# Query and gate products of the sparse attention in one four-bank buffer, and two modulation steps moved

## The reference, cut to what matters

```
def mixer_a(x, w_in, w_o, positions):
    proj = x @ w_in                      # x is 256 x 2048
    q, k, v, gate, iq, ik, iw = jnp.split(proj, SPLITS_A, axis=-1)
    ...                                  # rotary positions, indexer, top-k, softmax attention: o
    return (o * jax.nn.silu(gate)) @ w_o
```

```
mod_l = (jax.nn.silu(c) @ w_ada[l] + b_ada[l])[:, None, :]
sh_a, sc_a, gt_a, sh_f, sc_f, gt_f = jnp.split(mod_l, 6, axis=-1)
```

## Time and profile before

| | us |
|---|---|
| median of 3 runs | 2222.39 |
| lowest, highest | 2218.21, 2222.41 |
| the profiled execution, its own time | 2220.76 |
| its span in the profile | 2219.0 |
| TensorE busy (share of the span) | 2169.6 (98%) |
| VectorE busy | 1539.7 (69%) |
| ScalarE busy | 1044.7 (47%) |

### The profile page before, as it was taken

One profiled execution on the slowest core, in us unless ns is written; L12 is line 12 of the kernel. 1 busy time (PEld: TensorE's weight loads), 2 busy tenths in 40 slices (PEclk: granted clock), 3 DMA queues, 4 the chain that ended last, 5 costly groups with the idle time before them and its releaser, 6 DMA issues.

```text
span 2219.0 us, 34255 instructions
## 1 busy us (share of the span) xinstructions
PE 2169.6 (98%) x14840; PEld 1979.5 (89%) x14840; DVE 1539.7 (69%) x1894; ACT 1044.7 (47%) x1124; POOL 42.2 (2%) x81
## 2 busy tenths in 40 slices
PE   6999999999999999999999999999999999999998
PEld 3798887999888888888888899999999998899998
DVE  3579987889897566665667877965677645655674
ACT  3355353334554345543454444545345436764353
POOL 0000100000000000000000000000000000000000
PEclk8999998999999999999999999999999999999999
DMA  9968865786675555555555454434544554345543
GB/s 405 403 247 321 325 264 209 284 324 228 264 287 211 188 189 190 188 189 190 189 190 201 160 190 152 171 134 157 185 170 177 186 190 171 133 155 188 179 164 132
DMA packets 64791, 470.48 MB, mean 212 GB/s; under 512 B 7200, under 2 KB 7200, under 8 KB 8320
## 3 DMA queue, kind: packets, MB, share of 16 engines
q1 hardware_dynamic: 55008, 398.16, 48.8%
q0 software_dynamic: 9488, 68.03, 8.0%
q10 hardware_dynamic: 144, 2.10, 0.2%
HBM read 466.16 MB, written 2.10 MB: 211 GB/s over the span
## 4 chain that ended last, share of the span: by engine, by line
PE 88%; DVE 7%; DMA 2%; ACT 1%; issue 1%; SPq 0%; DVEq 0%; ACTq 0%
PE acc L2198 59%; PE aux L2198 29%; DVE ada_acc L1182 2%; DVE lo L1162 2%; DMA raw<-stream 1%; DMA ada_raw<-stream 1%; ACT hi L488 1%; DMA ada_raw<-ada_stream 0%; PE aux L2754 0%; DVE conv_sum L1483 0%; DVE columns L1457 0%; DVE ada_acc L1179 0%; DVE rstd L2102 0%; DVE rstd L1305 0%; PE aux L2556 0%
## 5 line engine op out<-in xcount | busy, mean ns | idle before, releaser
L1162 DVE TENSOR_TENSOR lo<-raw,hi 128x2048 fp32r<-128x2048 f32 x337 | 769.8, 2288 | 422.5 <-ACT hi L488 422.1
L488 ACT ACTIVATE hi<-raw 128x2048 fp32r<-128x2048 f32 x337 | 643.2, 1911 | 681.6 <-PE acc L2198 499.8
L2198 PE MATMUL acc<-act_both,hi 128*128 128x256 f32 (+1 forms) x5696 | 871.1, 308 | 17.3 <-ACT hi L488 5.3
L2198 PEld LDWEIGHTS acc<-act_both,hi 128*128 128x128 f32 x5696 | 777.1, 193 | 70.5 <-issue 18.7
L2198 PE MATMUL acc<-act_both,lo 128*128 128x256 f32 x3408 | 454.0, 284 | 0.0
L2198 PEld LDWEIGHTS acc<-act_both,lo 128*128 128x128 f32 x3408 | 435.7, 193 | 7.3 <-issue 0.2
L2198 PE MATMUL aux<-act_both,hi 128*128 128x512 f32 (+1 forms) x1248 | 258.2, 355 | 0.0
L2198 PEld LDWEIGHTS aux<-act_both,hi 128*128 128x128 f32 x1248 | 207.6, 190 | 29.6
L1182 DVE SCALAR_TENSOR_TENSOR ada_acc<-ada_raw,silu_c,ada_acc 128x512 f32<-128x512 f32 x224 | 152.7, 744 | 1.4 <-DMA ada_raw<-ada_stream 1.2
L2198 PE MATMUL aux<-act_both,lo 128*128 128x256 f32 x1040 | 138.7, 283 | 0.0
L2198 PEld LDWEIGHTS aux<-act_both,lo 128*128 128x128 f32 x1040 | 134.3, 191 | 4.6 <-issue 0.2
(11 more groups left out here) (357 smaller groups left out, 1713.7 us busy)
## 6 DMA issues: line engine op xcount, KB each, us to landing
raw<-stream SPq DMA_DIRECT2D x361, 1024.0 KB, 4.8
ada_raw<-ada_stream POOLq DMA_DIRECT2D x64, 1024.0 KB, 5.5
ada_raw<-stream SPq DMA_DIRECT2D x12, 1024.0 KB, 12.5
x<-x_t SPq DMA_DIRECT2D x1, 2048.0 KB, 7.6
ctx<-ctx_t SPq DMA_DIRECT2D x1, 2048.0 KB, 19.9
x<-x_t ACTq DMA_DIRECT2D x1, 2048.0 KB, 10.1
out<-x SPq DMA_DIRECT2D x3, 512.0 KB, 7.6
p_raw<-p_t POOLq DMA_DIRECT2D x1, 512.0 KB, 3.7
```

What stands on the lines that cost most here:

```text
L488: nc.scalar.activation(HI[high_slot(c)][:, :], RAW[SLOT[c]][:, :], ACT.Copy).then_inc(hi_done, 1)
L1162: V.tensor_tensor(LO[SLOT[c]][:, :], RAW[SLOT[c]][:, :], HI[high_slot(c)][:, :].bitcast(F32), ALU.subtract)\
L2198: return TE.matmul(out, lhs, rhs, start=start, stop=stop, skip_group_check=True)
```

## The change

Layer a takes layer b's way. Its query groups 1 to 3 and gate groups 0 to 2 go through `one_buffer`; ScalarE's and VectorE's steps 16, 20, 24, 28, 32 and 36 take the tiles over with `sides_out` and `sides_in`; the tag-dependent branches fall away; `single` now counts six groups of layer a ahead of layer b's. The third gate group gets its SiLU in step 37 from a copy. In `ADA_STEPS` the entries 7 and 8 go and 30 and 31 come, so that every modulation chunk from the fifth to the 37th runs in a later step than before; by the rule of `REDUCE_AT` the sums of groups 9 to 12 move from chunks 12, 14, 16 and 18 to 13, 15, 17 and 20, and that of group 16 from 29 to 32.

```
-ADA_STEPS = sorted([4, 4, 5, 5, 7, 8, 10, 11] + [m for m in range(12, 43) if m not in (30, 31)] +
-                   [12, 13, 14, 15, 16, 17, 18, 20, 24, 27, 28])
+ADA_STEPS = sorted([4, 4, 5, 5, 10, 11] + list(range(12, 43)) + [12, 13, 14, 15, 16, 17, 18, 20, 24, 27, 28])
...
     def single(tag, n):
-        return n
+        return n if tag == "a" else n + 6
...
                 for m in range(42):
                     first(m)
-                    if apart and m == 12:
+                    if m == 12:
                         act_evac(gq, U[:, 0:4, :])
-                    if apart and m in (16, 20, 24):
+                    if m in (16, 20, 24):
                         sides_out(m // 4 - 4, U[:, m - 12:m - 8, :])
-                    if apart and m in (28, 32, 36):
+                    if m in (28, 32, 36):
                         sides_out(m // 4 - 4, U[:, KD + m - 28:KD + m - 24, :])
                     split(c0 + m + 2)
...
-                    if not apart and 12 <= m <= 24 and m % 4 == 0:
-                        g = m // 4 - 3
-                        act_evac(gq + g, U[:, 4 * g:4 * g + 4, :])
-                    if not apart and m in (28, 32):
-                        g = m // 4 - 7
-                        act_evac(gg + g, U[:, KD + 4 * g:KD + 4 * g + 4, :])
...
-                    if m == 35 or (apart and m == 37):
+                    if m in (35, 37):
...
-                    if m == 40 or (not apart and m == 36):
+                    if m == 40:
...
-                    if q4 < (3 if tag == "b" else 2):
+                    if q4 < 3:
...
                 for m in range(42):
                     first(m)
-                    if tag == "b" and m in (16, 20, 24):
+                    if m in (16, 20, 24):
                         sides_in(m // 4 - 4, U[:, m - 12:m - 8, :])
-                    if tag == "b" and m in (28, 32, 36):
+                    if m in (28, 32, 36):
                         sides_in(m // 4 - 4, U[:, KD + m - 28:KD + m - 24, :])
                     split(c0 + m + 2)
...
-            phase("q_a", 4, after=attend_a)
-            phase("gate_a", 4, after=attend_a)
+            projections("a", "q_a", "gate_a", attend_a)
```

More of the change, by code:

```diff
@@ L937, in mixer @@
                 gv, gq, gg = PH[v][1], PH[q][1], PH[gate][1]
-                apart = tag == "b"
                 def sides_out(w, dst):
```

## The result

| | before | after |
|---|---|---|
| median | 2222.40 us (2218.21 to 2225.91, 6 runs) | 2233.14 us (2230.06 to 2236.06, 6 runs) |
| ratio to the kernel before | | 1.0051 (95%: 1.0039 to 1.0063) |
| the profiled execution | 2220.76 us | 2236.06 us |

The change costs 0.5%, 10.7 us between the medians. The two profiled executions lie 15.3 us apart, and it is these 15.3 us that the traces can divide. The one of the kernel after is the longest of its six, 2.9 us over their median.

A forecast was written before the change was run, and what follows sets the result against it. TensorE, working in 98% of the span, was taken as the bound. Layer a's +25.6 us less 8 for modulation gave +17.6: 2238.4 us for the profiled execution, 2240 for the median, range 2227 to 2250.

The forecast's parts named there:

- waits at 16, 20: Layer a, chunks 16 and 20: TensorE waits 4.4 and 5.0 us for adds because VectorE's queue is behind.
- waits at 24, 28, 32: Layer a, steady handovers: VectorE's adds stand behind `maximum2`, which waits for scores; TensorE waits 2.2 us each, 6.6 in all.
- wait at 36: Layer a, step 36: ScalarE's copies stand behind `head_out`, so TensorE waits 1.8 us.
- slower clock: Layer a: four of six possible waits lower TensorE's clock, 3.1 us per fall, +12.4 us; bounds zero and six falls.
- shorter products: Layer a, six groups of four chunks: each chunk 0.19 us shorter, 4.6 us less in all (2.4 to 5.3).
- layer a: Handovers 17.8 us less 4.6 for products, plus 12.4 for clock falls: +25.6 us.
- modulation: First block: later chunks remove two waits for sums and two clock falls, partly lost before norms: -8 us (0 to -11.5).
- Rival 2: Layer a's handover is as smooth as layer b's, where TensorE was never seen waiting: 2209.8 us; chance 0.07.
- Rival 1: The clock stays up after all of layer a's handovers: 2227.6 us; chance 0.13.
- Rivals 3 and 4: 3: VectorE's queue swallows the modulation gain, 2248 us, chance 0.10; 4: only steps 16, 20, 36 cost, 2227.2 us, 0.06.

The follow-up runs named there:

- e3: The changed kernel with layer a's hand-over (VectorE's adds, ScalarE's copies) put ahead of everything else in steps 16 to 36: 2218.50 us, ratio 0.9994.
- e5: The changed kernel with only VectorE's adds put ahead of everything else in steps 16 to 36, ScalarE's order kept: 2222.07 us, one run.
- e4: As e3, with VectorE's adds of the first two wide groups moved into steps 15 and 19, ScalarE's copies of the second into 19: 2209.40 us, 0.9953.
- e6: The changed kernel with half of the rounds of the top-k choice left out, so other keys are chosen: 2225.24 us, one run.
- e12: e4 with the query rotations spread over steps 13, 14, 17, 20, 22, 24, 25 and 26: 2208.69 us, ratio 0.9942.
- e1: The kernel before with only the new list of modulation steps: 2213.99 us, ratio 0.9966.
- e10: The kernel before with modulation entries 7 and 8 kept and only the nine chunks of steps 24 to 29 moved one step later: 2214.07 us, 0.9958.
- e2: The changed kernel with the old list of modulation steps, so the wide groups alone: 2241.36 us, ratio 1.0090.
- e8: e4 with 6, 5 and 4 idle VectorE instructions ahead of the adds of steps 24, 28 and 32: 2226.42 us, one run.
- e9: e4 with query rotations moved from steps 17, 18 to 20, 21 and from 21, 22 to 22, 23: 2213.79 us, ratio 0.9967.
- e7: e4 with 4, 5 and 6 idle VectorE instructions ahead of the adds of steps 24, 28 and 32: 2228.61 us, one run.
- e11: e9 with the smaller modulation edit of e10 in place of the whole new list: 2217.64 us, ratio 0.9977.

## Why the prediction was right in its sign, point by point

| term | forecast | measured in the profiled execution |
|---|---|---|
| waits at 16, 20 | 4.4, 5.0 | 4.23, 4.70 |
| waits at 24, 28, 32 | 2.2 each | 1.92 each |
| wait at 36 | 1.8 | 1.54 |
| slower clock | 4 falls x 3.1 = 12.4 | 3 falls: 2.4 + 1.6 + 1.6 = 5.6 |
| shorter products | -4.6 | -2.7 |
| layer a | +25.6 | +19.1 |
| modulation | -8 | -6.6 |
| up to 170 us | 0 | +2.8 |
| sum, profiled execution | +17.6 | +15.3 |
| between the medians | +17.6 | +10.7 |

- **The waits held.** All six came at the places named and within 0.3 us of the sums of single rows. The steady ones were 0.3 shorter: from `maximum2` to the adds it took 1.32 us as in the earlier trace rows, but `maximum2` began 0.04 us after TensorE was free (1456.88 - 1.92 = 1454.96) and not 0.38 after. e3 and e5 show the mechanism, e4 and e6 that of chunks 16 and 20.
- **The step that was mis-sized is the price of one fall of the clock.** I took 3.1 us from the first block, where two waits came one after the other with short products between them; whether that is why a fall cost more there no run tested. Behind a single wait in a stretch of dense products it was 1.6 us in eleven cases and 2.2 to 2.4 in four. Their number was three where I took four, inside my bounds, and the split which I used (4.4 and 5.0 surely, 2.2 at the edge, 1.8 not) came out right. This term alone was 6.8 us too high, about all of the 6.5 by which layer a was over-estimated; the waits (1.6 too high) and the products (1.9 too much gain) nearly cancel.
- **The shorter products.** Where nothing waits (e12), layer a is 3.2 us shorter with 0.45 of wait in it, so 3.6 us for 24 chunks, 0.15 each against my 0.19. In the change itself 2.7 is what the sum leaves, since a group that starts behind a wait gains less: four chunks take 30.99 us with a wait of 1.92 where they took 29.57, which is 0.5 and not 0.76. The page's rule that I set against the trace (the Trainium skill, TensorE: Matmul & The Clock Gate, section Back-to-back issue gap), which the page gives for an isolated matmul, led to an estimate of 1.0 us for all 24. The 3.6 us of e12 disagree with it.
- **The modulation steps.** Gone are 13.2 us, 11.5 forecast; the early steps cost 0.7, as forecast. TensorE waited 0.80 and 1.69 us for the norm where I had 1.7 and 1.7. At the mark at 480 us the part had gained 13.2 - 0.7 - 3.5 = 9.0 us, my 9.1, but that is two misses that cancel: 1.7 more was gone than I had, and the norms gave back 3.5 where I had 1.7. By e1's ratio it is worth 7.5 us, by e10's 9.3. What I had not seen is a wait and slower products near 482 us in the kernel after: VectorE's last modulation chunk but one waits 2.87 us for its DMA. I took it for a result of the new list, but e2, with the old list, loses 2.8 us in the same stretch, and of the kernels with the new one e3, e4, e6, e8 and e12 gain 0.8 to 1.0 while e1, e9, e5 and e7 lose 0.9, 0.6, 3.0 and 4.5. So it goes with the execution and not with the list; what makes it come and go stays open.
- **Rival 2** (as smooth as layer b) fell, and e4 shows that its condition was the right one: with the adds ahead of what waits for scores, and VectorE not behind, the time is 2209.4, its 2209.8. That the times meet so closely is partly chance, since layer a gave 0.9 us there and not its 4.6. **Rival 1** fell: three of six waits slowed the products. **Rivals 3 and 4** fell too: e1 shows the modulation part at work, and the three steady waits were 1.92 us each.
- **Luck in the sum.** The range of 2227 to 2250 held 2233.14, but the median was 6.9 us under the forecast of 2240. The profiled execution, at 2236.06, came within 2.3 us of its 2238.4 only since it was a long one: the 2.8 us up to 170 us, where the code is the same, and the 2.4 us near 482 us are in no term of the forecast. Without them it would be 10.1 us longer than before, close to the 10.7 between the medians.

## What to carry to other kernels

When a buffer is handed over tile by tile, look at what stands ahead of the freeing instruction in its engine's written order: if that waits for something which the bound engine issues only after the products that fill the buffer, the bound engine waits each time, and moving four instructions ahead gives it back. An engine that was 4 us late for a place which nobody waited for becomes a 4 us wait as soon as somebody does, so read the lateness before adding a reader. A step in which a queue waits for a sum formed in the same step costs far more than its own idle time (two waits of 5.8 us on VectorE were 13 us on the bound engine). Moving the nine chunks around those two waits by one step, so that the waiting ones stand behind their sums, was enough.

## What the runs showed of the hardware

Whether the clock falls behind a wait went largely with the length of the wait in these traces: of eleven waits of 1.92 or 1.93 us before a wide chunk two were followed by slow products, of four of 2.73 or 2.74 us two, and of eleven between 3.19 and 4.70 us all. The loss is read from start to start against the same chunk without a fall (7.10 us, and 5.66 for chunk 16): 1.6 us in most, 2.2 to 2.4 behind that of 3.87 and three of the four of 4.2. The two of 2.73 us that cost nothing stand before chunk 20 (e3, e5), the two of 2.74 that cost 1.6 before chunk 24 (e9, e11). Both slow cases among those of 1.92 stand before chunk 32 (the change, e2), while e6 and e8 have the same wait there without a loss. Length alone does not decide: in the kernel before, waits of 1.06 and 0.94 us in the first block were followed by slow products, and waits of 1.2 and 0.9 us between 170 and 336 us were not (granted clock 1.00). What decides stays open.

The same code before the first difference ran between 1.7 us shorter and 5.2 us longer up to 170 us than in the one profile of the kernel before. In e11 the stretch from 170 to 336 us, also unchanged code, was 6.3 us longer. A single profile against a single profile is therefore no measure for a part of 7 us, unless the stretches are compared mark by mark.
